# A two-layer diffusion backbone on one core: the first layer's modulations as products with moving weights in four column groups

## The reference

```python
mods = SiLU(cond) @ w_ada + b_ada          # 1024 -> 6 * 1024, for each of the two streams
shift1, scale1, gate1, shift2, scale2, gate2 = split(mods)
h = rms_norm(x, gain1) * (1 + scale1) + shift1
heads = h @ w_in                            # pooling, neighbourhood attention, gated linear attention
x = x + gate1 * (concat(A, B, C) @ w_out)
h2 = rms_norm(x, gain2) * (1 + scale2) + shift2
x = x + gate2 * (silu(h2 @ w_g) * (h2 @ w_u)) @ w_ffn_out
```

## Time and profile before

| | us |
|---|---|
| median of 3 runs | 1812.88 (1806.76 to 1815.16) |
| the profiled execution | 1812.43 |
| its span, from the first to the last instruction | 1810.6 |
| PE busy in it | 1708.4 (94%) |
| DVE busy in it | 1110.0 (61%) |

### The profile page before, as it was taken

The page is one execution under the profiler, slowest core; times in us unless marked ns, Lnnn a source line. Parts: engine busy times, 40 slices in busy tenths (PEclk is TensorE's granted clock), DMA queues, the critical chain, the costliest instruction groups (busy, mean ns, idle before and its releaser), DMA issues. The chain is left out here.

```text
span 1810.6 us, 28326 instructions
## 1 busy us (share of the span) xinstructions
PE 1708.4 (94%) x11552; PEld 1643.7 (91%) x11552; DVE 1110.0 (61%) x1997; ACT 556.3 (31%) x914; POOL 605.1 (33%) x288
## 2 busy tenths in 40 slices
PE   6889999988799999999999799999999999999998
PEld 6778888887799999999998788888999999999998
DVE  5686465769888788878665865656663423431342
ACT  2421354332322112212244225543432212221221
POOL 4135111124334343344353341111543333333332
PEclk9988899998899999999999979999999999999999
DMA  9111212124444344444322101121222222222213
GB/s 351 70 59 59 75 66 65 52 80 141 141 150 139 133 146 153 144 138 159 98 69 95 49 24 40 65 78 50 59 70 81 70 70 76 75 70 73 78 61 102
DMA packets 50869, 170.79 MB, mean 94 GB/s; under 512 B 6432, under 2 KB 9184, under 8 KB 50528
## 3 DMA queue, kind: packets, MB, share of 16 engines
q1 hardware_dynamic: 50784, 169.68, 28.7%
HBM read 165.86 MB, written 3.80 MB: 94 GB/s over the span
## 5 line engine op out<-in xcount | busy, mean ns | idle before, releaser
L537 POOL TENSOR_TENSOR w_lo<-w_raw,w_hi 128x1024 fp32r<-128x1024 f32 (+2 forms) x196 | 505.1, 2578 | 1054.7 <-ACT w_hi L634 1054.7
L634 ACT ACTIVATE w_hi<-w_raw 128x1024 fp32r<-128x1024 f32 (+2 forms) x194 | 200.0, 1031 | 673.4 <-PE acc L1304 610.1
L1304 PE MATMUL acc<-h_lo,w_hi 128*128 128x320 f32 x1472 | 339.4, 312 | 0.0
L1304 PE MATMUL acc<-h_hi,w_hi 128*128 128x320 f32 x1472 | 339.2, 312 | 0.0
L1304 PEld LDWEIGHTS acc<-h_hi,w_hi 128*128 128x128 f32 x1472 | 249.4, 190 | 1.4 <-issue 0.9
L1304 PEld LDWEIGHTS acc<-h_lo,w_hi 128*128 128x128 f32 x1472 | 249.3, 190 | 0.0
L1304 PE MATMUL acc<-y_hi,w_hi 128*128 128x320 f32 x896 | 209.9, 316 | 25.1 <-DVE x L1186 13.1
L1304 PE MATMUL acc<-h_hi,w_lo 128*128 128x320 f32 x1472 | 232.9, 310 | 0.0
L1304 PEld LDWEIGHTS acc<-h_hi,w_lo 128*128 128x128 f32 x1472 | 222.1, 189 | 0.0
L1304 PE MATMUL acc<-y_lo,w_hi 128*128 128x320 f32 x896 | 208.7, 315 | 0.0
L1304 PEld LDWEIGHTS acc<-y_hi,w_hi 128*128 128x128 f32 x896 | 154.0, 193 | 28.3 <-DVE y_lo L1246 13.6
(11 more groups left out here) (223 smaller groups left out, 2234.9 us busy)
## 6 DMA issues: line engine op xcount, KB each, us to landing
w_raw<-in_w SPq DMA_DIRECT2D x176, 512.0 KB, 3.5
mod_w<-in_w_ada SPq DMA_DIRECT2D x72, 512.0 KB, 3.7
bias<-in_bias SPq DMA_DIRECT2D x16, 576.0 KB, 4.6
w_ada<-in_w_ada SPq DMA_DIRECT2D x16, 512.0 KB, 9.4
w_raw<-in_w SPq DMA_DIRECT2D x16, 384.0 KB, 3.0
gate_w<-in_w_ada SPq DMA_DIRECT2D x8, 512.0 KB, 3.5
x<-in_x SPq DMA_DIRECT2D x1, 2560.0 KB, 15.4
out_x<-x SPq DMA_DIRECT2D x8, 320.0 KB, 3.8
```

Source lines behind the costliest of these rows:

```text
L537: pool.tensor_tensor(w_lo[p][:, 0:n], raw[p][:, 0:n], w_hi[p][:, 0:n].bitcast(F32), ALU.subtract).then_inc(lo_made[p], 1)
L634: act.activation(w_hi[p][:, 0:n], raw[p][:, 0:n], ACT.Copy).then_inc(hi_made[p], 1)
L1304: mm = pe.matmul(acc[p][:, half, 0:m.shape[-1]], w[:, k * P:(k + 1) * P], m, start=w is w_hi[p] and k == 0 and part is hi, stop=w is w_lo[ ...
```

## The change

1. **The products.** All of layer 0's shift1, scale1, gate1, shift2 and scale2 are now made on PE with the roles swapped: the two condition vectors, repeated to 32 columns, are the stationary side (128x32), and 128x128 of `w_ada` moves through. `row_products` takes two rows of `w_ada` (a pair) and has each write half of its blocks into each of two column groups of 32 (`tile_position`), four in all; 16 matmuls for a pair. The result is 4 x 32 partial rows in PSUM, which is copied to SBUF (DVE in the head, ACT's `move_products` in the steps), multiplied with a small selecting matrix (`turn_rows`, one matmul for a 128-channel pair column), and biased (DVE).
2. **The head.** DMA order: parameters, four rows of scale1, `x` in four parts, `T_LR`, four rows of scale1, `T_K`, eight rows of shift1, and the condition rows for DVE last. Gains are made for blocks 0 to 3 and 4 to 7 apart. DVE sums the squares, not POOL. PE does `T_LR` and `T_K` without the shift columns, then the four pairs of shift1, then `row_sums`, and then the shift columns of both tiles (`shift_products`, 48 matmuls of two columns).
3. **The steps.** The one-row gate products of steps 4 to 11 go; 12 pairs (gate1, shift2, scale2) stand at steps 0, 0, 1, 1, 4, 4, 5, 6, 7, 8, 9, 10 (`PAIR_STEP`), with four buffers (two pairs), and three groups of `turn_rows` at steps 4, 7, 11. The load of a pair waits until the pair two before it has been used. The context and bias loads move behind the last pair.
4. **DVE's rows.** Layer 0's `T_OUT` stage has none. The rest (56 rows) stands as before at two for each hidden tile of layer 0, four in the first chunk's output stage, and the last eight (layer 1's gate2) in layer 1's first chunk.
5. **The FFN's output product.** Its first tile is done block by block (`gemm`), the second by part, and a loop does the other six.

```diff
-ROW_SLOTS, COL_SLOTS = 7, 3
-FIRST_GATE_STEP = 4
+ADA_SLOTS, GM_SLOTS = 10, 4
+NMADE = GATE2 - GATE1
+PAIR_STEP = (0, 0, 1, 1, 4, 4, 5, 6, 7, 8, 9, 10)
+TURN_STEP = (4, 7, 11)
...
-    for m in range(KT):
-        at[T_OUT + m] = (len(rows), 2)
-        rows += [SCALE2 + m, SHIFT2 + m]
-    rest = list(range(GATE2, NMOD + NMOD))
+    rest = list(range(GATE2, 2 * NMOD))
...
+            take(0, start + 2 * j, 2)
+        if c == 0:
+            for m in range(0, KT, 2):
+                take(0, start + 2 * n + m, 1)
+    for j in range(KT):
+        take(1, T_FF + 2 * j, 1)
...
+            def load_ada(n):
+
+                if n >= ADA_SLOTS:
+                    sp.wait_ge(ada_used, (n - ADA_SLOTS) // 2 + 1)
+                row = SCALE1 + n if n < KT else SHIFT1 + n - KT
+                sp.dma_start(ada[n % ADA_SLOTS][:], a["w_ada"][row]).then_inc(ada_in[n % ADA_SLOTS], 16)
+
+            for n in range(KT // 2):
+                load_ada(n)
+            for i in range(KT // 2):
+                sp.dma_start(x[:, 2 * i:2 * i + 2, :], a["x"][:, 2 * i:2 * i + 2, :]).then_inc(x_in[i], 16)
+            sp.dma_start(raw[T_LR][:], a["w"][T_LR]).then_inc(raw_in[T_LR], 16)
+            for n in range(KT // 2, KT):
+                load_ada(n)
+            sp.dma_start(raw[T_K][:], a["w"][T_K]).then_inc(raw_in[T_K], 16)
+            for n in range(KT, 2 * KT):
+                load_ada(n)
             for m, t in (("rope", rope), ("causal", causal), ("heads4", heads4), ("edges", edges),
                          ("inv_w", inv_w), ("state", state_in)):
                 sp.dma_start(t[:], a[m]).then_inc(late_in, 16)
+            sp.dma_start(cond_rows[:], a["cond_rows"]).then_inc(rows_in, 16)
...
+                def load_pair(q):
+
+                    if q >= 2:
+                        sp.wait_ge(gm_used, q - 1)
+                    for r in (2 * q, 2 * q + 1):
+                        sp.dma_start(gm[r % GM_SLOTS][:], a["w_ada"][GATE1 + r]).then_inc(gm_in[r % GM_SLOTS], 16)
...
+                    for q in range(NMADE // 2):
+                        if l == 0 and t == (T_Q if q < 2 else T_PAIR + 2 + product_at(PAIR_STEP[q - 2]) // MMS):
+                            load_pair(q)
+                    if t == (T_K if l else T_PAIR + 4):
                         if l:
-                            sp.wait_ge(mod_used, 2 * (KT + len(LATE_ROWS)))
+                            sp.wait_ge(free["O"], 1 + l * len(FILLS["O"]))
+                            sp.wait_ge(mod_used, 2 * (len(LATE_ROWS) - KT))
+                        else:
+                            sp.wait_ge(gm_used, NMADE // 2)
...
+            def row_parts(b1, n1, b2, n2, to, rows, n):
+
+                dve.wait_ge(full[b1], after(b1, n1, 0))
+                link(dve.tensor_copy(to[:, 0:n * CHUNK], bank[b1][:, 0:n * CHUNK]))
+                dve.sem_inc(free[b1], 1)
+                dve.wait_ge(full[b2], after(b2, n2, 0))
+                return add_bias(rows, n, turned(b2, n))
+
...
-            link(add_bias(SCALE1, KT, acc[0][:, 0, 0:2 * KT].rearrange("p (m s) -> p m s", s=2)))
-            gains(0, 0, 0, KT).then_inc(gains_made, 1)
+            row_parts("S", "a1", "P", "a2", means1, SCALE1, KT // 2).then_inc(free["P"], 1)
+            dve.wait_ge(free["P"], 1 + after("P", "a2", 0))
+            gains(0, 0, 0, KT // 2).then_inc(gains_made, 1)
+            add_squares(0, KT - 1)
+            for k in range(KT // 2):
+                scaled_low(0, 0, k)
+            row_parts("O", "b1", "X", "b2", vT, SCALE1 + KT // 2, KT // 2).then_inc(free["X"], 1)
+            dve.wait_ge(free["X"], 1 + after("X", "b2", 0))
+            gains(0, 0, KT // 2, KT // 2).then_inc(gains_made, 1)
+            for k in range(KT // 2, KT):
+                scaled_low(0, 0, k)
+            row_parts("S", "c1", "P", "c2", vT, SHIFT1, KT).then_inc(free["P"], 1)
+            dve.wait_ge(free["P"], 1 + after("P", "c2", 0))
+            dve.sem_inc(shift_made, 1)
+            dve.wait_ge(h_hi_made, KT + 1)
+            dve.tensor_tensor(h_lo[:, :, T:TE], mods[:, SHIFT1:SHIFT1 + KT, :], h_hi[:, :, T:TE].bitcast(F32),
...
-                if l:
-                    gains(l, 1, 0, KT)
+                gains(l, 1, 0, KT)
                 for m in range(KT):
-                    late_mods(T_OUT + m)
-                    if l == 0:
-                        gains(l, 1, m, 1)
...
+            def row_products(to, n, pair_w):
+
+                for kk in range(KT // 2):
+                    for m, w in enumerate(pair_w):
+                        for e in range(2):
+                            k, quarter = 2 * kk + e, 32 * (2 * m + e)
+                            mm = pe.matmul(to[quarter:quarter + 32, n * P:(n + 1) * P],
+                                           cond[:, k, :], w[:, k * P:(k + 1) * P],
+                                           start=kk == 0, stop=kk == KT // 2 - 1, tile_position=(0, quarter))
+                return mm
+
+            def turn_rows(to, src, n):
+
+                for i in range(n):
+                    mm = pe.matmul(to[:, 4 * i:4 * i + 4], src[:, i * P:(i + 1) * P], sel, start=True, stop=True)
+                return mm
+
+            def first_pairs(b, first, n):
+
+                for i in range(n):
+                    pair_w = []
+                    for r in (2 * (first + i), 2 * (first + i) + 1):
+                        pe.wait_ge(ada_in[r % ADA_SLOTS], 16 * (r // ADA_SLOTS + 1))
+                        pair_w.append(ada[r % ADA_SLOTS])
+                    row_products(bank[b], i, pair_w).then_inc(ada_used, 1)
+                pe.wait_ge(ada_used, first + n)
+                pe.sem_inc(full[b], 1)
+
             pe.wait_ge(cond_made, 1)
-            for n in range(KT):
-                slot = ROW_SLOTS + n % COL_SLOTS
-                pe.wait_ge(ada_in[slot], (n // COL_SLOTS + 1) * 16)
-                for k in range(KT):
-                    mm = pe.matmul(acc[0][:, 0, 2 * n:2 * n + 2], ada[slot][:, k * P:(k + 1) * P], cond[:, k, :],
...
+                def no_shift(part):
+                    return lambda k, half: part[:, k, halves[half]]
+
+                def shift_products(p):
+
+                    for k in range(KT):
+                        for w, part in ((w_hi, h_hi), (w_hi, h_lo), (w_lo, h_hi)):
+                            mm = pe.matmul(acc[p][:, 1, HALF:HALF + 2], w[p][:, k * P:(k + 1) * P], part[:, k, T:TE],
+                                           start=False, stop=k == KT - 1 and w is w_lo)
+                    mm.then_inc(tile_done[p], 1)
+
...
+                    gemm_by_part(1, h(h_hi), h(h_lo), slot_uses(l, T_K))
+                else:
+                    ready(T_LR)
+                    gemm(0, no_shift(h_hi), no_shift(h_lo), wait_k=h_is_made(0), done=False)
+                    ready(T_K)
+                    gemm(1, no_shift(h_hi), no_shift(h_lo), done=False)
+                    first_pairs("S", KT // 2, KT // 2)
+                    pe.wait_ge(free["S"], 1 + after("S", "c1", 0))
+                    turn_rows(PT, vT, KT // 2).then_inc(full["P"], 1)
+                    row_sums(0)
+                    pe.wait_ge(h_made, KT + 1)
+                    for p in range(2):
+                        shift_products(p)
                 pe.wait_ge(layer_in, (l + 1) * 32)
                 pe.wait_ge(row_made, 1 + evacs(l, T_LR) + 1)
                 both_halves("S", "P", "zf", wgate[:, 0:P], lrT)
...
+                    for q in range(NMADE // 2):
+                        if l == 0 and g == PAIR_STEP[q]:
+                            pair_w = []
+                            for r in (2 * q, 2 * q + 1):
+                                pe.wait_ge(gm_in[r % GM_SLOTS], 16 * (r // GM_SLOTS + 1))
+                                pair_w.append(gm[r % GM_SLOTS])
+                            if q % 4 == 0:
+                                claim("P", f"g1_{q // 4}")
+                            row_products(PT, q % 4, pair_w).then_inc(gm_used, 1)
+                            if q % 4 == 3:
+                                pe.wait_ge(gm_used, q + 1)
+                                pe.sem_inc(full["P"], 1)
+
...
+                def out_stage(start, kts, made):
+
+                    ready(start)
+                    gemm(0, h(y_hi), h(y_lo), kts=kts, wait_k=lambda k: pe.wait_ge(hid_lo, 1 + l * NHID + made + k + 1))
+                    ready(start + 1)
+                    gemm_by_part(1, h(y_hi), h(y_lo), slot_uses(l, start + 1), kts)
+                    stage(start + 2, KT - 2, y_hi, y_lo, kts)
```

247 lines of the change are left out of this document (111 added, 136 removed).

## The result

The changed kernel takes 1757.8 us (median of 4 runs, 1755.4 to 1759.4) against 1814.0 for the kernel before on the same chip (4 runs, 1806.8 to 1817.4): ratio 0.970, 95% interval 0.968 to 0.973. Forecast were 1757 us. The total is right, but two of the five stretches behind it are off by more than 4 us, one to each side.

The account below looks back on a forecast made before the run. PE, busy 94% of the span, was taken as the bound, with little left in waits. The terms: 1812.4 - 11.2 + 6 - 6 - 32.9 - 10.5 = 1757.8, stated as 1757 us; range 1736 to 1786.

Parts of the forecast that it names:

- Layer 0's `T_OUT` stage: Last transpose before `T_OUT` to the row sums: falls from 90.8 us to layer 1's 57.8, -32.9 us.
- The y blocks: FFN output stages: with the first tile block by block, PE's waits for `y_lo` shrink, -10.5 us (bounds 0 and 12).
- The head: Start to `zf`: `T_LR` starts at 27.4 and `zf` comes at 59.7 instead of 70.9, -11.2 us.
- the shift products are hidden under the root's chain: Head, row sums to `zf`: 48 two-column products of 5.5 us fit under the inverse root's 7.8 us.
- Steps 0 to 3: Four added pairs (4.0 us) and load waits of 1.9 and 1.6, less slack: +6 us (bounds 0 and +8).
- The slack on DVE: Step 2: transposes take about 1 us from 110.06, DVE takes them at 112.38, so 1.3 us of delay is free.
- Steps 4 to 12: Gate rows go, eight pairs and twelve turns come: 73.3 us against 79.1, -6 (bounds -1 and -14).
- the rival of the denser products: Steps 4 to 12: denser products keep PE at 2.4 GHz, up to 17 us, half makes 1748; chance 0.13.
- the 5 us that I let hide: Steps 4 to 12: 5 us of the added pairs and turns fall under PE's idle time from DVE's chain.
- the rival of the longer steps: Pairs wait for DMA and hold bank P, nothing hides, eight steps lose 2 us each: near 1777; chance 0.13.
- The price of a pair: A pair's 16 matmuls on PE take 1.0 us, 2.0 at the low level, judged from L1543's 16 ns a record.
- The rivals with serial pairs: Column groups don't overlap: 6.2 us a pair at low level, 1838, chance 0.03; 3.1 at full clock, 1786, chance 0.05.

Follow-up runs that it names:

- no_out_rows: The kernel before without the 16 scale2 and shift2 rows made in layer 0's output stage (filled with a constant): 1781.9 us, ratio 0.982.
- y_in_order: The changed kernel with the first tile of each of the six FFN output stages by weight part again: 1774.7 us, ratio 0.979.
- head_order: The changed kernel with DVE copying the sums of scale1 rows 4 to 7 after the low parts of blocks 0 and 1: 1758.2 us, ratio 0.969.
- short_pairs: The changed kernel with only the last four of sixteen matmuls in the eight pairs of steps 4 to 10: 1757.9 us, ratio 0.970.
- one_group: The changed kernel with a pair's 16 matmuls ordered so that neighbours share their column group: 1774.4 us, ratio 0.979.
- two_groups: The changed kernel with a pair's 16 matmuls ordered so that neighbours alternate between two column groups only: 1765.6 us, ratio 0.974.

## Why the prediction was right, and where it was not

- **Layer 0's `T_OUT` stage** (-32.9): right, and shown twice, by the trace (57.81 us) and by `no_out_rows`. Layer 1 was a measured model of it. The term left out what the late row sums did to the stage behind them: after PE's pause of 7.60 us it took 485.63 - 478.81 = 6.8 us to the second FFN tile, at a clock of 0.58 in the first 5.2 of them, and now takes 443.74 - 439.08 = 4.7. These 2.2 us stand in the FFN's row of the table.
- **The y blocks** (-10.5): mis-sized. The waits were sized rightly: they fell by 10.2 us. What the term left out is the low clock behind a wait. The FFN stretches moved by -16.0 us; without the 2.2 us above it is -13.8, of which 3.1 us are the tails of the two waits of 2.02 us, and some 0.5 have no place. `y_in_order` gives back 16.5 us, since four of its waits have a tail and not two.
- **The head** (-11.2): -8.3, or -9.1 in the second profile. The failed step is "the last pair at the low level 2.0, DVE's copy 0.4, two turns 0.9, hand-offs 0.3, and PE starts `T_LR` at 27.4". The pair took its 2.0, but its rows were there at 25.1 and not at 23.8, so that it ended at 27.03, 1.2 us late. Then DVE was in the middle of 5.1 us of low parts, and the copy stood behind them in program order: it came at 29.79, 2.8 us late. Together 3.8 us were lost. 0.8 came back, since from the end of the row sums to `zf` it took 7.0 us where I had 7.8. `head_order` shows that putting the copy right alone gains nothing, because of the clock. That the shift products are hidden under the root's chain was not quite right: they took 7.0 us and not 5.5, since the last ones ran at the low level (0.21 us each instead of 0.11), and the chain took 6.3 (55.53 to 61.87) and not 7.8, since POOL was no longer in DVE's way. So the products end last, by 0.7 us.
- **Steps 0 to 3** (+6): +10.4, beyond its bound of 8. The four pairs took 1.95 + 1.08 + 1.69 = 4.7 us, the waits 3.4 as forecast (1.9 and 1.6; measured 2.00 and 1.44). Missing is the low level in `zf` and its neighbours, 67.15 - 62.60 = 4.55 us where before took 2.32, so 2.2; these sum to 10.3. The sum is not complete: the low level from 93.98 to 97.67 in the kernel before (1.6 us) is gone, and some 0.9 us of it are new behind pair 3. The slack on DVE that I had set off against the waits did help, but only behind the mark of the table: the transposes came 2.0 us later, DVE's copy of them 0.35. Up to that copy the stretch grew by 8.7.
- **Steps 4 to 12** (-6): -8.8 for the longer stretch from step 2 on, -7.1 from DVE's copy on. The clock rose from 0.86 to 0.92 in this stretch; PE's 117.5 us of work would be 117.5 x 0.92 / 0.86 = 125.7 at the old clock, so by this estimate the rival of the denser products has up to 8 us of it. Against that less was hidden under PE's waits than the 5 us that I let hide: PE's idle time grew from 7.8 to 11.5 us (the new wait of 3.6 us for bank P is in it, as the rival of the longer steps had it), and `short_pairs` says the same. No run separates the two shares.
- **The price of a pair** (1.0): 0.93 to 1.08 at the high level, 1.94 at the low one; right, and `one_group` and `two_groups` show that the four column groups make it so. The rivals with serial pairs fell, and their price was set too high (3.1; measured 2.46 with neighbours in one column group).

So the mechanism was right in the largest term, in the price of a pair and in the waits of the FFN. In the head it had DVE's order and the engine that ends last wrong. That the total came within 1 us is luck: the stretches are off by +2.9, +4.4, -2.8 and -5.5 us, and layer 1's mixer by +1.0, and these cancel. Part of them has one root: the sum went by waits and durations at the high level, and took the clock as given.

## What to carry to other kernels

Where another layer or stage runs the same work without the suspect, use its measured length as the forecast; it held to 0.1 us. A wait on a matmul engine that is otherwise dense can cost more than its length, since the products behind it may start at the low clock: here waits of 2.0 us cost 3.5, and those of 1.7 us nothing beyond themselves. So a small gap closed can gain more than its length, and time won in a part that is already ragged may be taken back. When small products are packed into column groups, let neighbours in the program go round all groups, and order the work of the engine that takes the sums over by when the sums are ready.
